# Pooled sums between the steps of a recurrence, and four small products among eight equal ones

## The reference, cut to what matters

```python
z = h @ w_in[l]                       # pool 512 | rx 1024 | rg 1024 | gates 2048 columns
# pool_mixer: four groups of 128 channels, windows 2, 4, 8, 16
mean = (sum over the last w positions) / min(t + 1, w)
d = mean - u
y_pool = (einsum('bsgc,gcd->bsgd', d, pool_w) * pool_scale) @ w_pool_out
# rg_lru_branch
xc = causal_dwconv(u_rx, conv_w, conv_b)            # 4 taps
r, i = sigmoid(xc @ w_gates + b_gates)              # 16 heads of 64, so block diagonal
log_a = -8 * r * softplus(-lru_lambda)
hs = recurrence(a = exp(log_a), u = sqrt(-expm1(2 * log_a)) * i * xc)
y_rnn = (hs * gelu(u_rg)) @ w_rg_out
merged = sigmoid(..) * y_pool + sigmoid(..) * y_rnn
```

## Time and profile before

| | us |
|---|---|
| median of 3 runs (lowest, highest) | 3487.85 (3486.68, 3489.31) |
| profiled execution, its own time | 3490.16 |
| its span in the trace | 3488.3 |
| TensorE busy in the span | 3179.9 (91%) |
| VectorE busy in the span | 2186.2 (63%) |
| ScalarE busy | 1312.6 (38%) |
| GpSimd busy | 1000.7 (29%) |

### The profile page before, as it was taken

One profiled execution on the slowest core, in us unless ns is written; L12 is line 12 of the kernel. 1 busy time (PEld: TensorE's weight loads), 2 busy tenths in 40 slices (PEclk: granted clock), 3 DMA queues, 4 the chain that ended last, 5 costly groups with the idle time before them and its releaser, 6 DMA issues. The chain is left out here.

```text
span 3488.3 us, 44976 instructions
## 1 busy us (share of the span) xinstructions
PE 3179.9 (91%) x15137; PEld 2526.0 (72%) x15137; DVE 2186.2 (63%) x2689; ACT 1312.6 (38%) x1717; POOL 1000.7 (29%) x501
## 2 busy tenths in 40 slices
PE   5889989788889499999959999699899999999998
PEld 4658867565677488888848788578668888888877
DVE  6588885677543899999965655743365235235366
ACT  3245423566412388888831265100131000000142
POOL 2323332000142011111114333245324444444432
PEclk9999999899999799999979999799999999999999
DMA  6313221231151699999961122032221111111312
GB/s 225 76 44 91 79 54 49 73 121 37 49 165 63 256 380 380 378 379 385 365 253 51 61 76 82 28 100 91 84 90 48 49 48 48 48 48 48 105 40 67
DMA packets 351491, 446.15 MB, mean 128 GB/s; under 512 B 32990, under 2 KB 235660, under 8 KB 351380
## 3 DMA queue, kind: packets, MB, share of 16 engines
q1 hardware_dynamic: 336676, 410.08, 34.5%
q10 hardware_dynamic: 5344, 17.83, 1.6%
q0 software_dynamic: 9360, 16.80, 1.3%
HBM read 397.40 MB, written 58.75 MB: 131 GB/s over the span
## 5 line engine op out<-in xcount | busy, mean ns | idle before, releaser
L410 PE MATMUL acc<-Ah,whi 128*128 128x512 f32 x2336 | 935.8, 401 | 80.0 <-DVE Al L604 21.4
L411 PE MATMUL acc<-Al,whi 128*128 128x512 f32 x2336 | 918.2, 393 | 0.0
L412 PE MATMUL acc<-Ah,wlo 128*128 128x512 f32 x2336 | 917.9, 393 | 0.0
L382 POOL TENSOR_TENSOR whi<-wraw,one 128x1024 fp32r<-128x1024 f32 (+2 forms) x208 | 390.0, 1875 | 1833.9 <-PE acc L412 1514.5
L410 PEld LDWEIGHTS acc<-Ah,whi 128*128 128x128 f32 x2336 | 443.7, 190 | 204.9 <-issue 71.1
L384 POOL TENSOR_TENSOR wlo<-wraw,whi 128x1024 fp32r<-128x1024 f32 (+2 forms) x208 | 530.1, 2548 | 16.3
L411 PEld LDWEIGHTS acc<-Al,whi 128*128 128x128 f32 x2336 | 444.2, 190 | 96.3 <-issue 5.6
L412 PEld LDWEIGHTS acc<-Ah,wlo 128*128 128x128 f32 x2336 | 443.2, 190 | 95.0
L1861 DVE TENSOR_TENSOR mlo<-mraw,mhi 128x1024 fp32r<-128x1024 f32 x256 | 307.0, 1223 | 38.0 <-ACT mhi L1810 22.8
L1810 ACT ACTIVATE mhi<-mraw 128x1024 fp32r<-128x1024 f32 x256 | 268.1, 1062 | 78.9 <-PE acc L1755 53.6
L410 PE MATMUL acc<-Bh,whi 128*128 128x512 f32 x640 | 251.3, 393 | 8.9 <-POOL wlo L384 8.9
(11 more groups left out here) (497 smaller groups left out, 4760.3 us busy)
## 6 DMA issues: line engine op xcount, KB each, us to landing
mraw<-in_exp_w SPq DMA_DIRECT2D x512, 256.0 KB
mraw<-in_exp_w SPq DMA_DIRECT2D x128, 512.0 KB, 11.6
wraw<-in_w_in SPq DMA_DIRECT2D x72, 512.0 KB, 3.7
wraw<-in_w_up SPq DMA_DIRECT2D x48, 512.0 KB, 3.8
TT<-in_ada_w SPq DMA_DIRECT2D x32, 512.0 KB, 3.8
TT<-gates SPq DMA_DIRECT2D x32, 512.0 KB, 4.5
wraw<-in_w_down SPq DMA_DIRECT2D x24, 512.0 KB, 3.9
adaraw<-in_ada_w SPq DMA_DIRECT2D x16, 512.0 KB
```

The costliest lines, as they stand in the source:

```text
L382: ch(pool.tensor_tensor(whi[:, r, 0:k, 0:m], wraw[:, r, 0:k, 0:m], one[:, 0:1].unsqueeze(2).broadcast_to([P, k, m]), ALU.mult))
L410: pe.matmul(o, whi[:, r, j, 0:m], ih[:, k0 + j, cols], start=(j == 0), stop=False)
L411: pe.matmul(o, whi[:, r, j, 0:m], il[:, k0 + j, cols], start=False, stop=False)
L412: last = pe.matmul(o, wlo[:, r, j, 0:m], ih[:, k0 + j, cols], start=False, stop=(j == k - 1))
```

## The change

Three things are moved.

1. The rate's tiny steps run after the convolution's tile 0, and `low(0)` after tile 1 (semaphore `xc` is set after tile 0 instead of tile 7).
2. The pooled sums are cut into 18 units of one or two VectorE instructions; recurrence tile j runs three of them, two after `gate_raw(j, 0)` and one after the difference of the logarithms. The division by the window is folded into the subtraction. The units work in `TT[0]` and `TT[1]`. VectorE's loop over tiles 0 to 6 is written out.
3. The pooled weights are loaded by one transfer of 256 KB, ahead of the `rx` weights on SyncE, into `pwr`, and split by GpSimd into `pwh`, `pwl` after the `rx` splits. The list `ITEMS` now has eight `rg` tiles. The small products follow `rg` products 1 to 4, go to the PSUM tiles `Y` and `XX` in turn, and are read by VectorE in rounds 2 to 5.

```diff
-         ... ("rg", 4), ("pw_rg", 8), ("mix", 16), ...
+         ... ("rg", 8), ("mix", 16), ...
+    pwr = alloc("pwr", [P, 4, P], F32, offset=o_bh + 20480)
+    pwh = alloc("pwh", [P, 4, P], F32R, offset=o_bh + 22528)
+    pwl = alloc("pwl", [P, 4, P], F32R, offset=o_bh + 24576)
...
+        sp.dma_start(pwr[:], A["pool_w_2"][0].rearrange("g p n -> p g n")).then_inc(S("pw_in"), 16)
         load_run(sp, N0["rx"], 8, in2(512))
         load_run(sp, N0["g2"], 16, in2(2560))
-        load_run(sp, N0["rg"], 4, in2(1536))
-        for g in range(4):
-            n = N0["pw_rg"] + 2 * g
-            load(sp, n, 0, A["pool_w_2"][0, g].rearrange("p (a n) -> p a n", a=1), k=1)
-            load(sp, n + 1, 1, W2[:, :, 1536 + (4 + g) * P:1536 + (5 + g) * P])
+        load_run(sp, N0["rg"], 8, in2(1536))
...
+        split_run(pool, N0["rx"], 8)
+        pool.wait_ge(S("pw_in"), 16)
+        ch(pool.tensor_tensor(pwh[:], pwr[:], one[:, 0:1].unsqueeze(2).broadcast_to([P, 4, P]), ALU.mult))
+        ch(pool.tensor_tensor(pwl[:], pwr[:], pwh[:].bitcast(F32), ALU.subtract))
+        pool.sem_inc(S("pw_split"), 1)
+        split_run(pool, N0["g2"], 16)
+        split_run(pool, N0["rg"], 8)
...
-        product_run(pe, N0["rg"], 4, Ah, Al)
-        for g in range(4):
-            n = N0["pw_rg"] + 2 * g
+        def pooled_product(g):
             pe.wait_ge(S("d_lo"), g + 1)
-            product(pe, n, 0, Bl2, Bl, 1, g, free=take(0))
-            product(pe, n + 1, 1, Ah, Al, free=take(1))
+            if g >= 2:
+                pe.wait_ge(S("py_lo"), g - 1)
+            for h in range(2):
+                o = (Y, XX)[g % 2][:, h * HALF:(h + 1) * HALF]
+                ... (3 matmuls: pwh, pwh, pwl)
+            last.then_inc(S("py_ps"), 1)
+
+        pe.wait_ge(S("ri"), 9)
+        pe.wait_ge(S("pw_split"), 1)
+        for j in range(KD):
+            product(pe, N0["rg"] + j, j % 2, Ah, Al, free=take(j % 2))
+            if 1 <= j < 5:
+                pooled_product(j - 1)
...
+        def widen(g, d, k):
+            s = TT[:, 1 - k, :] if d > 1 else UP[:, g, :]
+            ch(dve.tensor_copy(TT[:, k, 0:d], s[:, 0:d]))
+            ch(dve.tensor_tensor(TT[:, k, d:], s[:, d:], s[:, 0:T - d], ALU.add))
+
+        def pooled_unit(i):
+            if i >= 18:
+                return
+            g = (0, 0, 0, 1, 1, 1, 1, 2, 2, 2, 2, 2, 3, 3, 3, 3, 3, 3)[i]
+            step = i - (0, 3, 7, 12)[g]
+            s = TT[:, g % 2, :]
+            if step == 0:
+                dve.wait_ge(S("u_out"), g + 1)
+                ch(dve.tensor_tensor(UP[:, g, :], UP[:, g, :], R3, ALU.mult))
+            elif step <= g + 1:
+                widen(g, 2 ** (step - 1), (step - 1) % 2)
+            else:
+                ch(dve.tensor_tensor(s[:, 0:16], s[:, 0:16], pfix[:, g, :], ALU.mult))
+                ch(dve.scalar_tensor_tensor(UP[:, g, :], s, 1.0 / POOL_WINDOWS[g], UP[:, g, :], ALU.mult, ALU.subtract))
+                dve.sem_inc(S("pooled"), 1)
...
-        dve.sem_inc(S("xc"), 1)
-        (the nine tiny steps, wait for bd_in, low(0))
+            if j == 0:
+                dve.sem_inc(S("xc"), 1)
+                recurrence_rate()
+            if j == 1:
+                dve.wait_ge(S("bd_in"), 64)
+                low(0)
...
         def tile(j, last):
             gate_raw(j, 0)
+            pooled_unit(3 * j)
+            pooled_unit(3 * j + 1)
             dve.wait_ge(S("ri"), j + 2)
...
             dve.sem_inc(S("log_diff"), 1)
+            pooled_unit(3 * j + 2)
             dve.wait_ge(S("mult"), j + 1)
...
+        def pooled_out(g):
+            dve.wait_ge(S("py_ps"), g + 1)
+            if g == 0:
+                dve.wait_ge(S("gates2_st0"), 16 * 9)
+            (the three instructions of L2233 to L2236, now from (Y, XX)[g % 2])
+
         for j in range(KD):
             (read the rg product, set rg_raw)
+            if 2 <= j < 6:
+                pooled_out(j - 2)
             dve.wait_ge(S("rg_out"), j + 1)
             (multiply with the recurrence)
+            if j < 4:
+                dve.wait_ge(S("d_hi"), j + 1)
+                ch(dve.tensor_tensor(Bl[:, j, :], UP[:, j, :], Bl2[:, j, :].bitcast(F32), ALU.subtract))
+                dve.sem_inc(S("d_lo"), 1)
             (low part of the product)
-            (in rounds 0 to 3: pooled(j), wait for d_hi, the low part Bl)
```

More of the change, by code:

```diff
@@ L105 @@
 ITEMS = [("iq", 4), ("keys", 1), ("dviwfl", 1), ("gates", 16), ("fv", 4), ("qkd", 12), ("proj", 16), ("wout", 8),
-         ("pool", 4), ("rx", 8), ("g2", 16), ("rg", 4), ("pw_rg", 8), ("mix", 16), ("wo", 8),
+         ("pool", 4), ("rx", 8), ("g2", 16), ("rg", 8), ("mix", 16), ("wo", 8),
          ("ffn0", 24), ("ffn1", 24), ("ffn2", 24), ("plep", 2), ("pleg", 8)]
@@ L1980, in _ @@
                 pool.sem_inc(S("bd_zero"), 1)
-        for name, n in (("rx", 8), ("g2", 16), ("rg", 4)):
-            split_run(pool, N0[name], n)
-        for g in range(4):
-            for r in range(2):
-                n = N0["pw_rg"] + 2 * g + r
-                split(pool, n, r, landed[n], (1, KD)[r])
+        split_run(pool, N0["rx"], 8)
[5 more added lines that the diff above has]
+        split_run(pool, N0["rg"], 8)
     @block.tensor
@@ L2072, in _ @@
         taken[1] += 8
-        product_run(pe, N0["rg"], 4, Ah, Al)
-        for g in range(4):
-            n = N0["pw_rg"] + 2 * g
+        def pooled_product(g):
             pe.wait_ge(S("d_lo"), g + 1)
-            product(pe, n, 0, Bl2, Bl, 1, g, free=take(0))
-            product(pe, n + 1, 1, Ah, Al, free=take(1))
+            if g >= 2:
+                pe.wait_ge(S("py_lo"), g - 1)
+            for h in range(2):
+                o = (Y, XX)[g % 2][:, h * HALF:(h + 1) * HALF]
+                cols = slice(h * HALF, (h + 1) * HALF)
+                pe.matmul(o, pwh[:, g, :], Bl2[:, g, cols], start=True, stop=False)
+                pe.matmul(o, pwh[:, g, :], Bl[:, g, cols], start=False, stop=False)
+                last = pe.matmul(o, pwl[:, g, :], Bl2[:, g, cols], start=False, stop=True)
+            last.then_inc(S("py_ps"), 1)
[5 more added lines that the diff above has]
+                pooled_product(j - 1)
     @block.scalar
@@ L2130, in _ @@
         for j in range(KD):
+            if j < 4:
+                act.wait_ge(S("pooled"), j + 1)
+                act.activation(Bl2[:, j, :], UP[:, j, :], ACT.Copy).then_inc(S("d_hi"), 1)
             act.wait_ge(S("rg_raw"), j + 1)
@@ new lines, in recurrence_rate @@
+        def recurrence_rate():
+            dve.wait_ge(S("lru_ln"), 1)
+            ch(dve.tensor_scalar(z, e, 1.0, 1.0, ALU.add, ALU.subtract))
+            ch(dve.tensor_scalar(z, z, 1e-30, None, ALU.max))
+            ch(dve.reciprocal(z, z))
+            ch(dve.tensor_tensor(z, z, e, ALU.mult))
+            ch(dve.tensor_scalar(z, z, 2.0, None, ALU.min))
+            ch(dve.tensor_tensor(l, l, z, ALU.mult))
+            ch(dve.tensor_scalar(z, lam, -1.0, 0.0, ALU.mult, ALU.max))
+            ch(dve.tensor_tensor(l, l, z, ALU.add))
+            ch(dve.tensor_scalar(sp8[:, 0, :], l, LRU_C, None, ALU.mult))
@@ L2162, in _, with low @@
+        def low(j):
+            weights = bdr[:, :, ds(j, 1), :].rearrange("p g a n -> p g (a n)")
+            ch(dve.tensor_copy(bdh[:], weights))
+            ch(dve.tensor_tensor(bdl[:], weights, bdh[:].bitcast(F32), ALU.subtract))
+            dve.sem_inc(S("bd_split"), 1)
+            dve.wait_ge(S("xc_hi"), j + 1)
+            ch(dve.tensor_tensor(Bh[:, 1, :], row(C, j), Bh[:, 0, :].bitcast(F32), ALU.subtract))
+            dve.sem_inc(S("xc_lo"), 1)
         for j in range(8):
@@ L2219, in _ @@
         dve.sem_inc(S("lru"), 1)
[L2220 to L2225, removed]
         dve.wait_ge(S("fix_in"), 16)
-        for r in range(2):
-            dve.wait_ge(S(f"gates2_st{r}"), 16 * 9)
         for j in range(KD):
[L2230 to L2238, removed]
+            tile(j, j == KD - 1)
+        def pooled_out(g):
+            dve.wait_ge(S("py_ps"), g + 1)
+            if g == 0:
+                dve.wait_ge(S("gates2_st0"), 16 * 9)
+            ch(dve.tensor_scalar(TT[:, 2, :], (Y, XX)[g % 2][:], vec("pool_scale_2", g), None, ALU.mult))
+            ch(dve.tensor_copy(Bl[:, g, :], TT[:, 2, :]))
+            ch(dve.tensor_tensor(Bl2[:, g, :], TT[:, 2, :], Bl[:, g, :].bitcast(F32), ALU.subtract))
+            dve.sem_inc(S("py_lo"), 1)
+        for j in range(KD):
             u = TT[:, j % 2, :]
-            dve.wait_ge(w_used, n + 1)
-            ch(dve.tensor_tensor(u, acc[r][:], R3, ALU.mult))
-            dve.sem_inc(acc_free[r], 1)
+            dve.wait_ge(w_used, N0["rg"] + j + 1)
+            ch(dve.tensor_tensor(u, acc[j % 2][:], R3, ALU.mult))
+            dve.sem_inc(acc_free[j % 2], 1)
             dve.sem_inc(S("rg_raw"), 1)
+            if 2 <= j < 6:
+                pooled_out(j - 2)
             dve.wait_ge(S("rg_out"), j + 1)
@@ L2249, in _ @@
             dve.sem_inc(S("lru_lo"), 1)
```

4 lines of the change are left out of this document (1 added, 3 removed).

## The result

The changed kernel takes 3439.62 us (median; 3437.67 to 3441.26), the kernel before 3488.58 us on the same chip: a ratio of 0.986, with a 95% interval of 0.9848 to 0.9872. That is 49.0 us less; the forecast was 49.9 us less and 3438.0 us. The profiled execution took 3440.75 us, against 3490.16 us: 49.4 us less.

What follows compares the result with a forecast made beforehand. The prediction took TensorE's work and its gaps to bound the kernel. Gains of 42.0 + 8.6 = 50.6 us, less 0.7 us for seams, took 49.9 us off 3487.85 us: 3438.0 us, range 3434.5 to 3441 us.

Steps and rivals of the forecast that it cites:

- The eight `rg` and four small products: After the recurrence: 408 matmuls in 92.5 us, not 134.50; 42.0 us gained, 30.7 of waits and 11.3 of slower clock.
- The rounds: Beside the `rg` products: VectorE's round takes 10.3 us against TensorE's 12.2 us; `d_lo` comes some 3 us early.
- The early part: Convolution to first gates: the wait for `low(0)` and the slow clock behind it go, 8.6 us gained.
- The seams: Small waits at the seams, 0 to 1.5 us, for which 0.7 us was taken off the gain.
- The place of the ring: Recurrence: with the units, `gate_raw(j, 1)` ends at most 26.0 us after the tile's gates; TensorE needs its accumulator at 27.2.
- the ring: Recurrence: VectorE and ScalarE's chain from one `gate_raw(j, 1)` to the next, put at 22.4 us against TensorE's 24.48 us.
- What VectorE waits for it isn't added up.: Recurrence: GpSimd's time is fixed by TensorE, so VectorE's lateness from splits stays steady from tile to tile.
- Rival A: Recurrence: VectorE loses to a second split, `gate_raw(j, 1)` 1.2 us late in six tiles; 3445 us, up to 3461; chance 0.16.
- Rival D: Recurrence: every unit lies in the ring, stretched to 3.4 us, making the kernel slower: 3510 us; chance 0.01.
- B: Rounds are late: `d_lo` 3 us late at each of four small products, costing 20 us: 3458 us; chance 0.06.
- C: Early hole stays: first gates still wait for something after the convolution, 42.0 us remain gained: 3446.6 us; chance 0.04.
- E: Whole change: it doesn't do what it says, the same waits return under other names: 3488 us; chance 0.01.

Runs made afterwards that it cites:

- experiment 3: Changed kernel with the pooled weights back in the weight buffers, the pooled sums staying in the recurrence: 3457.58 us.
- experiment 4: Changed kernel with the pooled sums back in rounds 0 to 3, the pooled weights staying outside the weight buffers: 3473.06 us.
- experiment 5: Changed kernel with one idle VectorE pass behind the third unit in each of the eight tiles: 3443.54 us.
- experiment 9: Changed kernel with the third unit ahead of the wait for the logarithms and one idle pass in the place it left: 3441.74 us.
- experiment 7: Changed kernel with four idle VectorE passes behind the third unit in each of the eight tiles: 3506.24 us.
- experiment 11: Changed kernel with one idle VectorE pass behind the first two units, ahead of the wait for the sigmoids, in all eight tiles: 3437.58 us.
- experiment 2: Changed kernel with the early part undone, rate steps and `low(0)` behind the whole convolution again: 3446.85 us.
- experiment 6: Changed kernel with two idle VectorE passes behind the third unit in each of the eight tiles: 3460.32 us.
- experiment 8: Changed kernel with the third unit of each tile ahead of the wait for the logarithms, no idle pass: 3438.37 us.
- experiment 10: Changed kernel with the third unit ahead of the wait for the logarithms and two idle passes in the place it left: 3452.79 us.

## Why the prediction was right, point by point

- **The eight `rg` and four small products, 42.0 us.** Right: 134.50 us have become 92.5 us, the waits are gone and the clock share is 1.00. Experiments 3 and 4 show that it needs both edits. Of the 11.3 us that the prediction puts down to the clock, some 9.8 us are matmuls that start more slowly; the rest lies in the gaps, which are longer from start to start than the waits table says.
- **The rounds.** Right. Round 3, to set beside the earlier trace rows:

```profile
2197.75 1.23 DVE L2268 TENSOR_TENSOR TT<-acc,RG 128x1024 f32<-128x1024 f32 x1 [1.89 <-PE acc L415]
...
2205.49 1.22 DVE L2278 TENSOR_TENSOR Bl<-UP,Bl 128x1024 fp32r<-128x1024 f32 x1
2206.87 1.23 DVE L2281 TENSOR_TENSOR Cl<-C,Bh 128x1024 fp32r<-128x1024 f32 x1
```

  It takes 10.35 us to the end of the low part (10.3 us forecast), and `d_lo`, at 2206.71, is 3.1 us ahead of its small product at 2209.79 ("some 3 us").
- **The early part, 8.6 us.** Right: the gates follow at once, the 12 matmuls take 2.72 us. `low(0)` fits where it stands; the next product's reading is idle for 0.27 us before it instead of 2.50 us:

```profile
1899.78 1.22 DVE L2204 TENSOR_TENSOR Bh<-C,Bh 128x1024 fp32r<-128x1024 f32 x1
1901.27 1.23 DVE L2211 TENSOR_TENSOR TT<-acc,RG 128x1024 f32<-128x1024 f32 x1 [0.27 <-PE acc L415]
```

- **The seams, 0.7 us.** Not there: 50.6 us in the trace. With the 0.7 us back and the 1.2 us off by which the profiled run was late ahead of the change, 49.9 us become the 49.4 us of the profiled run. That the time came so near is in part luck, as the four runs of the changed kernel spread over 3.6 us; the 50.6 us of the stretch are the firmer figure.
- **The place of the ring, 26.0 us after the gates.** The end was right, 25.3 to 25.7 us in tiles 1 to 5, TensorE never held, the second `rg` product included (0 to 0.5 us forecast). The margin is 1.6 us, where 1.2 us were forecast. The path there was somewhat off: the late pattern had the rate step at 9.4 and the difference ready at 16.2, behind the start of `wlo`. They come at 8.8 and 15.5, so the difference catches the end of `whi` ("2 to 3 us later" is 1.4 us), and the third unit pays the split in its place. That VectorE's loop over the tiles is written out was undone by no run. It can't have given TensorE time by itself, as TensorE waited nowhere in tiles 1 to 7 before; but the steps of the ring are a little shorter with it (0.22 us from scan to `gate_raw`, 0.30 us), and what share of the slack is owed to it isn't shown.
- **"What VectorE waits for it isn't added up."** This sentence was wrong as a rule, though it did no harm here. It holds only while the ring, with the waits in it, keeps within 24.48 us. That the end repeats itself tile by tile was right for the changed kernel, and one pass more undoes it: then the end moves by 1.2 us a tile (experiment 5), in the other order by some 0.5 us (experiment 9), and with four passes the waits are paid in full (experiment 7).
- **Rival A**'s outcome, TensorE held a little in several tiles, was therefore nearer than a margin of 1.2 us in the end of a tile suggests: one pass more behind the difference, and TensorE waits in five places. Its mechanism, a waiting pass that a second split overtakes, isn't what did it: in none of the traces does a waiting pass of VectorE see a second split begin before its turn, and the most that one loses between 1845 us and `mix` is 2.1 us. **Rival D**'s side, slower than before, is reached only between two and four passes added (3506.24 us at four); its condition, all units in the ring, is not met, for two of three lie in the 9 us of experiment 11. **B, C** and **E** are excluded by the waits; C's price, 3446.6 us, is what experiment 2 measured (3446.85 us).

What VectorE and GpSimd do to each other here, the Trainium skill, "SBUF — State Buffer", section "Who interferes with whom", tells as an exclusive lock that whoever issued first keeps for its whole instruction. The traces agree, also for 16 columns (2.15 us for 0.17 us) and for the scan (4.31 us for 2.29 us).

## What to carry to other kernels

Ask of every idle stretch which chain ends it. Work put where an engine waits for a chain that doesn't pass through it is free (experiment 11). In the ring the same passes cost little at first and then more than their own time: 5.6, 24.0 and 69.6 us for 10, 20 and 40 us of work (experiments 5 to 7). So two margins are wanted, and not one: how far the ring's end is ahead of the need, which is spent once, and how far the whole ring, with its waits, is under the period, which counts in every tile. Adding idle passes measures the second, which the place of the ring's end in one tile doesn't show. Where two causes hold the same engine, undo them one by one and together: each hid part of the other, and what they cost one by one (18.0 and 33.4 us) didn't sum to the whole (42.0 us). An order that is no faster but leaves 3.2 us to spare instead of 1.6 us (experiment 8) is the better one to build on.

## What the runs showed of the hardware

- A pass of 16 columns with two inputs in SBUF, 0.17 us by itself, took 2.15 us behind a split by GpSimd. A copy of 4 columns, with one input in SBUF, took 1.78 us in tile 5 of the changed kernel, and ended with the split that began at 2090.97 and took 2.40 us. `gate_raw`, which has one input in PSUM, took 1.22 to 1.23 us in all tiles of all these kernels, beside splits too.
- After a gap of 3.15 us (experiment 3) TensorE lost 0.1 us of clock over the next 48 matmuls in one case of four, and 1.5 to 1.6 us in three. In experiment 10 gaps up to 1.25 us cost 0.1 us, one of 2.14 us 1.7 us, and of two gaps of 3.05 us one 0.1 us and the other 1.7 us. The first matmul behind the gap doesn't tell which it will be: in experiment 3 it lasted 0.50 us in the cheap case and 0.80 us in the others, but behind both gaps of 3.05 us it lasted 0.47 us. What decides stays open.
